# Score products of both halves of a differential attention head issued alternately, as one group

## What is computed

```python
def diff_attend(q, k, v, lam):
    s = jnp.einsum('bqhjd,bshjd->bhjqs', q, k).astype(jnp.float32)
    p = jax.nn.softmax(s, axis=-1)
    a = (p[:, :, 0] - lam * p[:, :, 1]).astype(v.dtype)
    return jnp.einsum('bhqs,bshe->bqhe', a, v)
```

## Time and profile before

| | us |
|---|---|
| median of 3 runs | 4348.33 |
| lowest and highest | 4346.35, 4352.66 |
| the profiled execution | 4349.23 |
| its span on the core | 4347.4 |
| PE busy | 3881.6 (89%) |
| PE weight loads | 3150.1 (72%) |
| DVE busy | 2204.2 (51%) |
| ACT busy | 1662.0 (38%) |
| the four differential heads | about 195 (4.5% of the span) |

### The profile page before, as it was taken

One profiled execution on the slowest core, in us unless ns is written; L12 is line 12 of the kernel. 1 busy time (PEld: TensorE's weight loads), 2 busy tenths in 40 slices (PEclk: granted clock), 3 DMA queues, 4 the chain that ended last, 5 costly groups with the idle time before them and its releaser, 6 DMA issues.

```text
span 4347.4 us, 52378 instructions
## 1 busy us (share of the span) xinstructions
PE 3881.6 (89%) x18218; PEld 3150.1 (72%) x18218; DVE 2204.2 (51%) x3735; ACT 1662.0 (38%) x2456; POOL 53.2 (1%) x104
## 2 busy tenths in 40 slices
PE   7989978998999988999797767799998887788997
PEld 5878866876878866878585655688887676676885
DVE  4634457777643456777435554533323436645333
ACT  3333444323233344332426654422222336553222
POOL 0000000000000000001000000000000000000000
PEclk9999999999999999999897867999999987789998
DMA  3262313454221322446110000111111110112222
GB/s 117 90 99 83 107 63 112 143 168 146 92 76 56 107 97 73 143 135 215 51 63 5 0 0 7 37 63 63 62 63 53 63 34 0 26 41 65 95 92 72
DMA packets 117851, 334.42 MB, mean 77 GB/s; under 512 B 38127, under 2 KB 38895, under 8 KB 117103
## 3 DMA queue, kind: packets, MB, share of 16 engines
q1 hardware_dynamic: 83087, 269.06, 19.9%
q0 software_dynamic: 14400, 52.44, 3.8%
q10 hardware_dynamic: 20256, 11.53, 1.0%
HBM read 330.89 MB, written 6.97 MB: 78 GB/s over the span
## 4 chain that ended last, share of the span: by engine, by line
PE 75%; DVE 11%; ACT 6%; issue 3%; DVEq 2%; DMA 2%; ACTq 1%; SPq 0%
PE PS L374 12%; PE PS L376 11%; PE PS L375 11%; PE PS L724 10%; PE PS L727 10%; PE PS L725 10%; PE PS L761 2%; PE PS L781 2%; PE PS L755 2%; PE PS L424 1%; PE PS L512 1%; DMA RAW<-in_stream 1%; DVE PTL L1999 1%; DVE PB L1478 1%; PE PS L521 1%
## 5 line engine op out<-in xcount | busy, mean ns | idle before, releaser
L1488 DVE TENSOR_TENSOR WL<-RAW,WH 128x1024 fp32r<-128x1024 f32 x494 | 604.3, 1223 | 575.2 <-ACT WH L939 571.4
L939 ACT ACTIVATE WH<-RAW 128x1024 fp32r<-128x1024 f32 x494 | 521.3, 1055 | 705.9 <-PE PS L727 368.3
L374 PE MATMUL PS<-HHI,WH 128*128 128x512 f32 x1632 | 659.0, 404 | 53.7 <-DVE HLO L1525 36.7
L376 PE MATMUL PS<-HHI,WL 128*128 128x512 f32 x1632 | 646.0, 396 | 0.0
L375 PE MATMUL PS<-HLO,WH 128*128 128x512 f32 x1632 | 645.6, 396 | 0.0
L724 PE MATMUL PS<-H2HI,WH 128*128 128x512 f32 x1472 | 530.0, 360 | 46.0 <-DVE H2LO L1938 34.7
L725 PE MATMUL PS<-H2LO,WH 128*128 128x512 f32 x1472 | 499.9, 355 | 0.0
L727 PE MATMUL PS<-H2HI,WL 128*128 128x512 f32 x1472 | 436.2, 356 | 0.0
L374 PEld LDWEIGHTS PS<-HHI,WH 128*128 128x128 f32 x1632 | 310.3, 190 | 142.8 <-issue 46.8
L724 PEld LDWEIGHTS PS<-H2HI,WH 128*128 128x128 f32 x1472 | 280.3, 190 | 125.3 <-issue 40.5
L376 PEld LDWEIGHTS PS<-HHI,WL 128*128 128x128 f32 x1632 | 310.9, 191 | 72.0
(11 more groups left out here) (275 smaller groups left out, 6386.0 us busy)
## 6 DMA issues: line engine op xcount, KB each, us to landing
RAW<-in_stream SPq DMA_DIRECT2D x494, 512.0 KB, 3.3
MODW<-in_modw POOLq DMA_DIRECT2D x96, 512.0 KB, 4.2
bias_rows<-in_rpb SPq DMA_DIRECT2D x1, 4762.5 KB, 56.8
BIAS<-bias_rows ACTq DMA_DIRECT2D x20, 224.0 KB, 4.0
MEM<-in_mem ACTq DMA_DIRECT2D x3, 1024.0 KB, 4.7
X<-in_x SPq DMA_DIRECT2D x1, 2048.0 KB, 9.1
CROW<-in_crow POOLq DMA_DIRECT2D x4, 512.0 KB, 4.6
out<-X SPq DMA_DIRECT2D x1, 2048.0 KB, 7.4
```

Of the source, the lines that this page charges most:

```text
L374: nc.tensor.matmul(out, WH[:, slot, b * P:(b + 1) * P], hi, start=start, stop=False)
L376: return nc.tensor.matmul(out, WL[:, slot, b * P:(b + 1) * P], hi, start=False, stop=stop)
L939: A(WH[:, d, :], RAW[:, s, :], ACT.Copy).then_inc(high_split, 1)
L1488: TT(WL[:, d, :], RAW[:, s, :], WH[:, d, :].bitcast(F32), ALU.subtract).then_inc(split_ready, 1)
```

## The change

In the differential heads PE's two score steps become one, `scores_of_both`. It issues the products of half 0 and of half 1 in turn (high by high of half 0, high by high of half 1, high by low of half 0, and so on): twelve for 768 keys and six for 256, the same ones as before. Each half's last product raises `s_done` as before. Of the two waits, one before each half's scores, one is left, for both exponentials of the block in progress. The first block's scores are issued in the same way. ACT's and DVE's code is unchanged, and so are the ordinary heads.

```diff
+                def scores_of_both(qb):
+
+                    q = slice(qb * P, (qb + 1) * P)
+                    o = 0
+                    for k0, k1 in ((0, T), (T, TA)) if qb < 4 else ((T, TA),):
+                        for x, (lq, rk) in enumerate(((qh, kh), (qh, kl), (ql, kh))):
+                            for half in range(2):
+                                rows = slice(half * HD, half * HD + HD)
+                                last = nc.tensor.matmul(FLAT[:, 2 * half * T + o:2 * half * T + o + k1 - k0], lq[rows, q], rk[rows, k0:k1],
+                                                        start=x == 0, stop=x == 2)
+                                if k1 == TA and x == 2:
+                                    last.then_inc(s_done, 1)
+                        o += k1 - k0
+
...
-                scores(0)
-                scores(1)
                 if diff:
+                    scores_of_both(0)
                     for qb in range(nq):
-                        for n in (2 * qb, 2 * qb + 1):
-                            m.add("exp")
-                            if n + 2 < 2 * nq:
-                                pe.wait_ge(exp_done, m.at("exp"))
-                                scores(n + 2)
+                        m.add("exp", 2)
+                        if qb + 1 < nq:
+                            pe.wait_ge(exp_done, m.at("exp"))
+                            scores_of_both(qb + 1)
                         m.add("comb")
                         pe.wait_ge(combined, m.at("comb"))
...
+                scores(0)
+                scores(1)
                 for n in range(2 * nq):
```

## The result

| | before | changed |
|---|---|---|
| median, us (6 runs each) | 4347.34 | 4363.87 |
| lowest and highest | 4344.16, 4352.66 | 4362.20, 4375.39 |
| profiled execution | 4349.23 | 4375.39 |
| its span | 4347.4 | 4373.6 |
| PE busy | 3881.6 | 3877.4 |

The account below looks back on a forecast made before the run. It took a chain of waits in the differential heads, handed on by DVE with PE's scores beside it, as the bound. Profiled 4349.2 + 19.3 delay + 2.2 clock = 4370.7, median 0.9 lower, said as 4370 us; range 4359 to 4383.

Parts of the forecast that it names:

- The sum: Differential heads: half 0's later start delays blocks 1 to 3 by 1.36, 1.73, 1.73 us; 4.82 a head, 19.3 in four.
- slack (0.13 us): Blocks 2 and 3: half 0's scores have 0.13 us to spare before their maximum, taken off the 1.86 us later start.
- a latency of 0.04 us: Score blocks where PE is last: 0.04 us from a product's end to the start of the maximum.
- The pairs: Twelve alternating score products: two matmuls on different halves cost one, so either half takes 2.29 us, as before.
- rival C: Score products: the halves don't run together, half 0 takes 1.85 us more in three blocks a head; 4394 us, 5 in 100.
- Rival B: Score blocks: PE's array time is the bound, so packing saves 1.85 us in twelve blocks; 4327 us, 2 in 100.
- Rival D: Half 0's scores were already started by something as late as half 1's, so no effect; 4348 us, 3 in 100.
- The short blocks: Blocks 4 and 5 (256 keys): value products already precede the scores, so the merged wait costs nothing.
- The clock: PE's clock changes fall elsewhere in longer heads: +2.2 us in all, ends -2.2 and +6.6.
- Rival A: Score blocks: both halves in use raise PE's clock to 2.4 GHz, shortening scores and transposes; 4346 us, 8 in 100.
- The argument against it: Score work becomes about 2.1 us between waits of 2 us or more; PE, busy without a break, still stays at 1.2.
- The total: Whole kernel: slower, 4370 us, with 82 in 100 given to this forecast.

Follow-up runs that it names:

- e4: Changed kernel with half 1's products issued ahead of half 0's instead of in turn, merged wait kept: 4383.07 us against 4344.83 before, ratio 1.0086.
- e1: Changed kernel with the merged wait kept but half 0's six products issued, then half 1's six: 4373.22 us against 4344.83 before, ratio 1.0060.
- e2: Kernel before with the change in blocks 4 and 5 (256 keys) of each head alone: 4348.44 us against 4348.13, ratio 0.9996.
- a2: The changed kernel run once more, unaltered, beside a repeat of the merged wait alone: 4365.00 us against 4349.15 before, ratio 1.0041.
- e1b: Repeat of e1, merged wait without alternation, beside a2 on the same chip: 4369.17 us against 4349.15 before, ratio 1.0044.
- f1: Changed kernel plus unneeded products in PE's idle time behind scores and transposes of the early blocks: 4347.34 us against 4344.83 before, ratio 1.0004.
- f2: Kernel before plus four unneeded 128-row products ahead of the transposes, behind the scores of blocks 1 to 3: 4351.32 us against 4344.83, ratio 1.0011.
- f3: Kernel before plus unneeded products on the other half's 64 rows beside scores of blocks 1 to 3: 4345.80 us against 4349.15, ratio 0.9995; again 0.9993.
- f4: f3 plus unneeded products beside scores of blocks 4 and 5, in later gaps and at the head's end: 4332.11 us against 4348.13 before, ratio 0.9962.

## Why the prediction was right, point by point

**The sum.** 1.36, 1.73 and 1.73 us a head were forecast. 1.34, 1.73 and 1.73 were measured in heads 2 to 4, with 1.24 for block 1 of the first head, where DVE and not PE had been last. 19.3 us forecast, 19.1 measured. The two terms that rested on slack (0.13 us) and on a latency of 0.04 us held to 0.02 us.

**The pairs.** 2.29 us for either half was taken from rows 3 and the pairs of rows 5; it was 2.29. Half 1 first (e4) shows side-by-side running from another side, and rival C is out.

**What costs.** The wait alone gives the change's distances (e1), so the alternation neither costs nor helps. Rival B (PE's time is the bound) is out with it: the change shortens PE's score work from 4.14 to 2.29 us a block and gets nothing for it, as PE had to wait 2.5 us for the combination instead. Rival D (half 0 was started by something late anyway) is out as well: its start moved, and block 3's distance with it, from 6.42 to 8.15 us.

**The short blocks** were costed at nothing, covered by value products. e2 bears it out.

**The clock** was the term that was mis-sized. +2.2 us was taken as the middle between the first head's and the second's clock; it was 4.8 in the profiled execution. In a2 the same three columns give 4.9, in e1 4.9 and in e1b 4.0, all against the one trace of the kernel before. The middle was the wrong choice: of the sixteen heads of these four traces twelve spend 1.7 us or more above the second head before in these columns, and one 1.3. The range had the room (to +6.6).

**Rival A** did not happen: 0.50 in the score blocks. But its price was right in blocks 2 and 3. With the clock raised by hand (f1) half 0's scores took 1.32 us for 1.30 forecast, the distances of blocks 2 and 3 are 0.09 us above those before (6.45 and 6.51 against 6.36 and 6.42) where 0.74 - 0.68 = 0.06 was forecast, while the time lay 2.5 us above its before where 3 below was forecast. Some 3.8 of these 5.5 us are block 1, which lost 1.3 us a head at the lower clock and not 0.37. The argument against it was half right: the pauses matter (f1 fills them). But it took it that PE is busy without a break at 1.2 GHz in the kernel before. Rows 6 show that for two single us; over 14 us it is busy for 11.29, and only f2 closes the gaps. What holds the clock down even then is, as f3 speaks for it, the idle rows.

**The total.** 4370 was forecast and 4363.9 measured, 21.7 us more and 16.5 (18.1 by the means), with the mechanism and its size as forecast. In the profiled execution the stage grew by 24 us and the span by 26; yet the medians differ by 16.5. The executions differ from one another before the stage even begins: the first maximum of head 1 comes at 2499.60 us in the trace of before, and at 2498.37 (the change), 2488.72 (a2), 2494.38 (e1) and 2494.11 (e1b) in the four traces with the merged wait, whose code up to there is that of before. Of all fourteen traces that of before comes there last. A span of one execution can be 10 us off by that alone. What makes this spread was not tried and stays open. The 19.1 us of the distances and 4.0 to 4.9 us of clock make a ratio of 1.0053 to 1.0055. That is inside the intervals of e1, a2 and e1b and at the upper end of the change's own. Part of how near the total came is luck: with the clock term that the traces show, the forecast would have been about 4372, further from 4363.9.

## What to carry to other kernels

When two steps are merged behind the later of two waits, ask who waits for the earlier step, and read from the timeline how far apart their starts are: here that distance, less the slack at the reader, was the price to 0.02 us, block by block. A faster or denser group on an engine that is off the chain brings nothing; it only makes the engine's idle time longer. Where an engine's clock depends on its use, half-height products can hold it at half speed while the busy share reads 100%, and unneeded products on the idle rows cost no time of their own (f3). They raised the clock, but by themselves they won nothing that shows (ratios 0.9995 and 0.9993); it took unneeded products in the gaps behind them as well to win 16 us (f4).

## What the runs showed of the hardware that I had not expected

- The granted clock differed with the rows in use, at a busy share that pointed the other way. 14.00 of 14 us busy, mostly with 64-row products, stayed at 0.50 (f2); 5.23 of 6 us busy at 0.50, with both halves of the rows, was followed by 0.97 over the next 14 us (f3). The Trainium skill, "TensorE: Matmul & The Clock Gate", under What's actually happening, speaks of how busy the engine has lately been; these windows show that the busy share of the profile alone doesn't tell it.
- A product on the other 64 rows costs nothing beside one that is running (both start at 2553.20 and at 2553.79 in f3), even with its own weight load. And without alternation the second half starts with the first half's third product, 1.02 us in (2572.20 to 2573.22 in e4), by itself. "TensorEngine Tiling (Array Packing)" in the Trainium skill says under Key Properties that tiles load and multiply in parallel, and the traces agree.
- The same code reached the stage at times up to 10.9 us apart in different executions (2488.72 in a2 and 2499.60 in before).
